# One block for routing and experts, and operands of three-pass products at multiples of 128 bytes

## The reference, cut to what matters

```
# first block
h = modulate(rmsnorm(x), ...);  proj = h @ w_in            # q k v g a p
o = gla_bidirectional(q, k, v, decays, states of a context of 256 tokens)
x = x + gate * (concat(rmsnorm(o) * silu(g), pooled p) @ w_out)
t = modulate(rmsnorm(x), ...)                              # 512 x 1024
group, experts = top 1 of 4 groups, top 2 of its 8 experts
for e in range(32):                                        # 1024 -> 2*256 -> 1024
    acc += ((silu(a) * u) @ w_expert_out[e]) * gates[e],   a, u = t @ w_expert_in[e]
x = rmsnorm(x + gate * acc)
# second block, layer 0, then layer 1
h = h + gdn_mixer(rms_norm(h))      # projection 1024 -> 4096 + 16, conv, gated delta rule, @ w_out
h = h + swiglu(rms_norm(h))         # 1024 -> 2 * 2816 -> 1024
k, v = rms_norm(h) @ w_kv;  h = h + stick_breaking(rms_norm(h) @ w_q, k, v) @ w_out
h = h + swiglu(rms_norm(h))
```

## Time and profile before

| | us |
|---|---|
| median of 3 runs | 2233.72 |
| the three runs | 2230.69, 10999.35, 2233.72 |
| the profiled execution | 2230.66 |
| its span in the profile | 2228.8 |
| TensorE busy | 1994.5 (89%) |
| VectorE, ScalarE, GpSimd busy | 996.6, 699.8, 335.5 |
| read from and written to DRAM | 285.10 MB, 14.71 MB |

### The profile page before, as it was taken

How to read it: one execution, slowest core, us unless ns; L and a number is a source line. 1 busy time by engine, 2 the same in 40 slices (tenths; PEclk the granted TensorE clock), 3 DMA queues, 4 the chain that set the end, 5 groups by cost and what they waited for, 6 DMA issues and landing times. The chain is left out here.

```text
span 2228.8 us, 28821 instructions
## 1 busy us (share of the span) xinstructions
PE 1994.5 (89%) x11270; PEld 1490.2 (67%) x11270; DVE 996.6 (45%) x1385; ACT 699.8 (31%) x1091; POOL 335.5 (15%) x264
## 2 busy tenths in 40 slices
PE   5988994977886999668899999999999889999999
PEld 2756762322225777567788888888677777888887
DVE  3431434211115567866454433333587445333333
ACT  2432231201103444334433322222542544222232
POOL 1332210211113344034321000000200001000000
PEclk9999996999998999889999999999999899999999
DMA  8137027899982222111002222232222012222221
GB/s 345 48 132 272 14 67 284 328 423 425 422 348 77 67 87 93 59 43 35 2 29 95 86 95 94 96 100 95 85 76 76 1 48 88 101 94 93 96 95 47
DMA packets 64276, 287.53 MB, mean 129 GB/s; under 512 B 10248, under 2 KB 11560, under 8 KB 54840
## 3 DMA queue, kind: packets, MB, share of 16 engines
q1 hardware_dynamic: 55376, 271.15, 33.0%
q0 software_dynamic: 6256, 11.03, 1.3%
q10 hardware_dynamic: 2552, 4.05, 0.5%
HBM read 285.10 MB, written 14.71 MB: 135 GB/s over the span
## 5 line engine op out<-in xcount | busy, mean ns | idle before, releaser
L308 PE MATMUL ps<-t_hhi,t_whi 128*128 128x512 f32 x768 | 304.8, 397 | 2.8 <-POOL t_wlo L2665 1.6
L310 PE MATMUL ps<-t_hlo,t_whi 128*128 128x512 f32 x768 | 304.7, 397 | 0.0
L309 PE MATMUL ps<-t_hhi,t_wlo 128*128 128x512 f32 x768 | 302.5, 394 | 0.0
L2463 DVE TENSOR_TENSOR t_wlo<-ring,t_whi 128x1024 fp32r<-128x1024 f32 x132 | 163.9, 1242 | 244.4 <-ACT t_whi L2459 244.4
L2459 ACT ACTIVATE t_whi<-ring 128x1024 fp32r<-128x1024 f32 x132 | 139.3, 1055 | 322.8 <-PE ps L310 322.8
L1513 PE MATMUL ps<-w_up,hgT 128*64 128x512 f32 x576 | 145.6, 658 | 45.0 <-DMA w_up<-experts 45.0
L308 PEld LDWEIGHTS ps<-t_hhi,t_whi 128*128 128x128 f32 x768 | 144.3, 188 | 40.6 <-DVE t_hlo L2729 3.7
L309 PEld LDWEIGHTS ps<-t_hhi,t_wlo 128*128 128x128 f32 x768 | 144.4, 188 | 35.6 <-issue 1.0
L310 PEld LDWEIGHTS ps<-t_hlo,t_whi 128*128 128x128 f32 x768 | 144.1, 188 | 33.1
L308 PE MATMUL ps<-t_ahi,t_whi 128*128 128x512 f32 x352 | 137.0, 389 | 0.0
L309 PE MATMUL ps<-t_ahi,t_wlo 128*128 128x512 f32 x352 | 137.0, 389 | 0.0
(11 more groups left out here) (556 smaller groups left out, 3725.1 us busy)
## 6 DMA issues: line engine op xcount, KB each, us to landing
ring<-stream SPq DMA_DIRECT2D x276, 512.0 KB, 3.3
w_up<-experts SPq DMA_DIRECT2D x36, 2048.0 KB
mix<-experts SPq DMA_DIRECT2D x18, 1024.0 KB, 20.6
hn<-experts SPq DMA_DIRECT2D x18, 1024.0 KB, 21.6
yrow<-y_dram SPq DMA_DIRECT2D x4, 1024.0 KB, 8.0
tab<-table POOLq DMA_DIRECT2D x1, 2528.5 KB, 12.3
res<-xT ACTq DMA_DIRECT2D x1, 2048.0 KB, 18.9
h_dram<-mix SPq DMA_DIRECT2D x4, 512.0 KB, 10.3
```

Source lines behind the costliest of these rows:

```text
L308: pe.matmul(out, w_hi, a_hi, start=start, stop=False)
L309: pe.matmul(out, w_lo, a_hi, start=False, stop=False)
L310: return pe.matmul(out, w_hi, a_lo, start=False, stop=stop)
L2463: ve.tensor_tensor(w_lo[:, j % 2, :], ring[:, (B0 + j) % SLOTS, :], w_hi[:, j % 2, :].bitcast(F32), ALU.subtract).then_inc(blocks_done, 1)
```

## The change

Two things are done.

**Places.** Two tiles that nothing reads are put in: `even_up`, 64 bytes, ahead of `hctx`, and `even_up_SS`, 64 bytes, ahead of `SS`. `ea` is 32 elements wide instead of 1, of which the first is used, and `t_kvlo` begins at the next multiple of 128. Then all operands of three-pass products lie at multiples of 128. Modulo 256 they are after the change: first projection 128 for all (the context's low part 0); o 128 for all; gdn 0, but `ring_lo` and `g_lo` 128; gdnout and sbout 128 against weights at 0; gu 0, but `t_hlo` 128; down 0 for all; q as gu; k and v 128 and 0 against weights at 0.

**One block.** The code of the experts' block moves into the first block, behind each engine's routing code. Between them stands a wait for `meta_ready`, which VectorE raises when the list of tiles is written. TensorE issues 28 products of `ident` and `ones` ahead of that wait. SP issues the first down weights only when both first gathers have landed. GpSimd raises `y_final` when all rows of the experts are stored, SP waits for it and loads `yrow` still inside the block; `yrow` now lies on `w_up`. The drain, the barrier and the branches at L1160 are gone; those at L1442 stay, now at the end of the one block.

```diff
+        def idle_products(pe, n, bank):
+            for _ in range(n):
+                pe.matmul(ps[:, bank, 0:P], ident, ones, start=True, stop=True)
...
         small_in = kept_sem("small_in")
+        sb("even_up", [P, 16])
         hctx = sb("hctx", [P, KT, CTX])
...
+        sb("even_up_SS", [P, 16], on=gla)
         SS = sb("SS", [P, 4, 12, P], on=gla)
...
+        meta_ready, y_final = sem("meta_ready"), sem("m_y_final")
+        rows_back = [kept_sem(f"rows_back{t}") for t in range(TT)]
+        yrow = over("yrow", [P, 2, TT, D], F32, "w_up")
...
                 sp.wait_ge(h_stored, TT * 16)
                 for s in range(2):
+                    sp.wait_ge(M["gathered"][s], 16)
+                for s in range(2):
                     for u in range(2):
                         sp.dma_start(w_down[s][:, u, :], experts[2 * s + u, :, KT * 512:]).then_inc(down_in[s], 16)
+                sp.wait_ge(meta_ready, 1)
+                later = sp.value_load(meta[0:1, MAXTILES + 1:MAXTILES + 2], min_val=NEXP // QUAD - 1,
...
+                sp.wait_ge(y_final, 1)
+                for t in range(TT):
+                    sp.dma_start(yrow[:, :, t, :], y_dram.rearrange("(a t p) d -> t p a d", a=2, p=P)[t]
+                                 ).then_inc(rows_back[t], 16)
...
                 m.then_inc(tok_found, 1)
+                idle_products(pe, 28, 0)
+                pe.wait_ge(meta_ready, 1)
...
                 for s in range(2):
                     pool.wait_ge(M["y_stored"][s], turns * 16 + 16)
+                pool.sem_inc(y_final, 1)
+                for s in range(2):
                     pool.wait_ge(M["gathered"][s], turns * 16 + 32)
...
                 step(ve.tensor_copy(meta[:, :], meta_f[:, :]))
+                ve.sem_inc(meta_ready, 1)
...
-        ea = sb("ea", [8, 1], on=gdn)
+        ea = sb("ea", [8, 32], on=gdn)
...
-        yrow = over("yrow", [P, 2, TT, D], F32, "Q")
...
-                for t in range(TT):
-                    sp.dma_start(yrow[:, :, t, :], y_dram.rearrange("(a t p) d -> t p a d", a=2, p=P)[t]
-                                 ).then_inc(rows_back[t], 16)
                 load_blocks(sp, STREAM["gdnout"].start + SLOTS)
...
-            kv_lo = over("t_kvlo", [P, KT, T], F32R, "tab", 32 * (-(-TABLES["level"].start // 8)))
+            dead = home["tab"] + 4 * TABLES["level"].start
+            kv_lo = over("t_kvlo", [P, KT, T], F32R, "tab", -(-dead // 128) * 128 - home["tab"])
```

More of the change, by code:

```diff
@@ L1233, in _, with turn_tokens, up @@
                 m.then_inc(tok_found, 1)
+                idle_products(pe, 28, 0)
+                pe.wait_ge(meta_ready, 1)
+                def turn_tokens(s):
+                    for k in range(KT):
+                        m = pe.transpose(ps[:, 2 + k // 4, (k % 4) * P:(k % 4 + 1) * P],
+                                         hg[:, s, k * P:(k + 1) * P], ident)
+                    m.then_inc(M["turned"][s], 1)
+                def up(s, part):
+                    for k in part:
+                        for u in range(2):
+                            m = pe.matmul(ps[half[u], s, :], hgT[:, s, k, half[u]],
+                                          w_up[:, s, u, k * 512:(k + 1) * 512], start=k == 0, stop=k == KT - 1)
+                    if k == KT - 1:
+                        m.then_inc(M["up_used"][s], 1)
@@ new lines, in turn_hidden, with down @@
+                def turn_hidden(i, s):
+                    pe.wait_ge(M["hid_done"][s], i + 1)
+                    for f in range(2):
+                        m = pe.transpose(ps[:, s, f * P:(f + 1) * P], hid[:, s, f * P:(f + 1) * P], ident)
+                    m.then_inc(M["hid_tr"][s], 1)
+                def down(s, f):
+                    for n in range(2):
+                        for u in range(2):
+                            m = pe.matmul(ps[half[u], 4 + 2 * s + n, :], hidT[:, s, f, half[u]],
+                                          w_down[s][:, u, f * D + n * 512:f * D + (n + 1) * 512],
+                                          start=f == 0, stop=f == 1)
+                    if f == 1:
+                        m.then_inc(M["down_used"][s], 1)
@@ new lines, in _ @@
+                for s in range(2):
+                    pe.wait_ge(M["gathered"][s], 16)
+                    if s:
+                        pe.wait_ge(M["turned_a"][0], 4)
+                        pe.wait_ge(M["turned_b"][0], 4)
+                    turn_tokens(s)
+                with pe.Fori(0, quads(pe)) as i:
+                    for s in range(2):
+                        pe.wait_ge(M["turned_a"][s], i * 4 + 4)
+                        pe.wait_ge(M["turned_b"][s], i * 4 + 4)
+                        pe.wait_ge(M["hid_kept"][s], i + 1)
+                        pe.wait_ge(up_in[s], i * 32 + 32)
+                        up(s, range(0, KT // 2))
+                        if s == 1:
+                            turn_hidden(i, 0)
+                        up(s, range(KT // 2, KT))
+                    for s in range(2):
+                        pe.wait_ge(M["hid_kept"][s], i + 2)
+                        pe.wait_ge(M["y_a"][s], i + 1)
+                        pe.wait_ge(M["y_b"][s], i + 1)
+                        pe.wait_ge(down_in[s], i * 32 + 32)
+                        down(s, 0)
+                        if s == 0:
+                            turn_hidden(i, 1)
+                        down(s, 1)
+                        pe.wait_ge(M["gathered"][s], i * 16 + 32)
+                        if s == 0:
+                            pe.wait_ge(M["turned_a"][1], i * 4 + 4)
+                            pe.wait_ge(M["turned_b"][1], i * 4 + 4)
+                        else:
+                            pe.wait_ge(M["turned_a"][0], i * 4 + 8)
+                            pe.wait_ge(M["turned_b"][0], i * 4 + 8)
+                        turn_tokens(s)
```

227 lines of the change are left out of this document (79 added, 148 removed).

## The result

The changed kernel takes 2223.34 us, median of 5 runs (2219.11 to 2227.46), against 2233.72 before: ratio 0.9961, 95% interval 0.9948 to 0.9974. That is 10 us less, where 30 were forecast, and outside the stated range. The profiled execution, at a span of 2225.6, is the slowest of the five; it lies 3.2 us under the span before.

A forecast was written before the change was run, and what follows sets the result against it. Most of the kernel was taken to go at TensorE's pace, the experts at their weights' transfers. 2230.7 − 9.0 − 4.2 − 14.8 = 2202.7, stated as 2204 because two of three runs shown were 3 higher; range 2192 to 2221.

The forecast's parts named there:

- First seam: Start of the experts: without block end, barrier and POOL's drain, the first reload of up weights goes out 9.0 us sooner.
- The gathers' 4.9 us: Start of the experts: gathers without down weights beside them land 4.9 us after issue, at 381.6 and 383.0.
- the down weights' cover: Start of the experts: down weights issued about 383 land about 393 to 395, wanted at 400.5; cover some 6 us.
- Second seam: End of the experts: yrow issued by 679.4 instead of 683.75, so the merge starts 4.2 us sooner; bounds −1.9 and −4.5.
- the drain lies beside the 4.9 us of landing: End of the experts: POOL's drain overlaps the landing of the early yrow loads, the first landing at 684.3.
- Pads: Three-pass products at moved places: shorter steps in gu, gdn, gdnout, sbout, q, k, v and first projection, together −14.8 us.
- I take 229 for the former: gu, gdn, gdnout, sbout, q, k and v, with operands 0 and 128 mixed modulo 256, step at 229 ns, not 233.3.
- the slow pace: Rival: gu, gdn and the rest go at 233.3 ns, first projection still gains 1.5; 2218.5 us, chance 0.22.
- Slower by collision: Rival: operands at one remainder modulo 256 or 512 get in each other's way at the new places; 2247.5 us, chance 0.04.
- Places do nothing: Rival: something other than operand places sets the products' pace, leaving −13.2 us alone; 2217.5 us, chance 0.13.
- The idle products overshoot: Rival at the experts' start: the clock stays at half and the 28 products end at 387.2; 2209.5 us, chance 0.08.

The follow-up runs named there:

- rows_after_gathers: The changed kernel with GpSimd raising y_final behind its waits for the last gathers, so the yrow loads go out later: 2216.31 us, ratio 0.991.

## Why the prediction was wrong

**First seam, −9.0 at the first reload: the mechanism right, the size short.** The products end at 383.7 (forecast 383.3), the transposes at full clock, the up products at 387.4 (386.7), the reload at 394.7 (393.8). The gathers' 4.9 us, taken from the yrow loads' row, came out at 4.8; that the two agree is luck, since the loads are of another kind and size. The term that was mis-sized is the down weights' cover: "landed about 393 to 395" by 4.2 MB at the full rate. The last landed at 397.6; the next two gathers and the reload were in the engines beside them. So the stretch bound by transfers began later than the reload's issue, and 6.0 are left at its end. Without the hold it is 3.9 (264.0 to 260.1).

**Second seam, −4.2: failed.** The step "the drain lies beside the 4.9 us of landing" held for yrow, but the working left out what else was on the queues: the last gather, of which the block's end makes a condition. The wait grew from 2.4 to 6.0 us and took back all but 0.4. `rows_after_gathers` shows it by putting the loads 2.2 us later, which starts the merge 3.9 us sooner against that gather. From the last gather to the merge it is then 7.5 us where it was 11.7: the 4.2 of the forecast, reached by issuing the loads later and not sooner. The prediction had asked what stands behind SP's waits and not what the loads, once early, collide with.

**Pads, −14.8: failed at "I take 229 for the former".** The profiled execution has gu at 232.0 and 233.5 and gdn at 233.3, near the rival called the slow pace, which was given 0.22; that rival's time, 2218.5, still was 5 us low: it kept the whole of both seams, 13.2, of which 6.6 were left at the merge. A second execution of the same kernel has gu at 229.9 and 229.1. Added up by steps over all large products, pauses left out, the pads brought some 0.5 us in the first and 7.5 in the second, nowhere 14.8; 4.1 of the 7.5 are the pace that gu1 drew. So the choice between two paces was the wrong question: there is no one pace at mixed places. The part of the reasoning that held is the table of remainders modulo 256: the first projection, alike after the change, reached 226.7 where it runs on without a pause, down stayed at 226.6, and the steady stretches of all others stayed out of that pace. The rule that row and table already bore, alike modulo 256 gives 226.7, was read as a remark on down and not as what decides; taken as the rule, it would have said that the change brings gu, gdn and the attention nothing sure.

**Slower by collision: excluded.** All operands at one remainder modulo 256 are the fastest case, at 0 (down in the changed kernel), 64 (o before), 96, 128 and 160. **Places do nothing: excluded**, by 128 bytes that move `t_alo` alone. **The idle products overshoot: did not come**, the transposes ran at full clock. The Trainium skill ("TensorE: Matmul & The Clock Gate", Step-by-step: what each phase is for) has it that the weight load does not take from the running product. The measurement differs: the same product takes 226.7 or some 234 ns by the place of one operand. Whether weight load and stream collide, or something else in reading them does, no run here shows.

**What is open.** Why the address has this effect, and what settles the pace at a pause. Also the clock, which takes and gives a few us where TensorE has short idle times: 2.5 us in the inversion in the changed kernel's profile, 1.4 ahead of o. The two profiles of the changed kernel are 11.2 us apart, 3.2 and 14.4 under the span before, though both begin the merge 6.5 or 6.6 us sooner than it. gu0 with q and gu1 make 6.6 of the difference by their pace. The attention makes 3.7: from the last product of v to the first of sbout it takes 85.9 us at a granted clock of 0.87 in the one and 82.2 at 0.95 in the other (86.1 at 0.87 before). The recurrence, from gdn's last product to gdnout's first, took 231.6 to 236.0 us in the fourteen profiles, at 0.91 to 0.87. So 6.5 us are won by the merge in both, and the rest goes by the pace and the clock that an execution draws.

## What to carry to other kernels

Where many products follow each other, give moving and held operands the same address modulo 256, whatever the value, and measure the distance of starts, not the record's length; a pace that differs between two executions, or ahead of a pause and behind it, at the same places is a sign that they are not alike. Don't judge such a kernel by one profile. Before a transfer is issued earlier, list what else is in flight then and who waits for it: a block's end can hang on a transfer whose data nobody needs. When a wait is taken out ahead of a stretch bound by transfers, count the gain where the stretch begins to move its bytes, and not where its first transfer is issued.

## What the runs showed of the hardware

- A chain of rounded 32-bit products of 512 columns, each with a weight load of its own, goes at 226.7 ns a step at full clock with all operands alike modulo 256 (at 0, 64, 96, 128 and 160), in all profiles. At mixed places it goes at 228.9, 231.1 or 233.3 in the steady stretches of gu.
- At mixed places the pace is settled anew at a pause and then held, in gu1 for 885 products: 233.3 and 231.1 in two executions of the kernel before, 233.3 and 228.9 in two of the changed one.
- Behind a pause the first products are slower even with all operands alike: in a block of p ten at 232 each, then 226.7.
- In down, `t_alo` 128 off slowed only the product that streams it (step 0.24 instead of 0.23), and `t_alo` 32 off slowed all three kinds (231.3 in the mean), in one profile each.
- A gather by index takes 2.2 to 2.4 us in nearly idle queues, 4.6 to 5.7 beside the last of the up weights, 8.4 to 9.0 beside up and down weights, and 6.0 beside 4 MB of yrow issued 0.24 us after it.
- GpSimd's drain at the block's end takes 3.3 to 3.5 us once the last gather has landed, in all profiles.
